# Feed-forward up projections as seven half products for eight, with each feed-forward in an up phase and a down phase

## What is computed

```python
h = x + concat(pool_mixer, rg_lru) @ w_out            # first block: mixer
h = h + square(relu(rms_norm(h) @ w_up)) @ w_down     # feed-forward one,   1024 -> 4096 -> 1024
h = h + sigmoid(rms_norm(h) @ w_ple_gate + b) * (p @ w_ple_proj)
h = rms_norm(h)
# second block
h = h + 0.5 * rms_norm((silu(a) * b) @ ffn1_w_out)    # a, b = split(rms_norm(h) @ ffn1_w_in), 1024 -> 2 x 2816
h = h + rms_norm(mixer(h))                            # dilated attention and an S5 state space model
h = h + 0.5 * rms_norm((silu(a) * b) @ ffn2_w_out)    # feed-forward three, like two
```

## Time and profile before

| | |
|---|---|
| median of 3 runs | 3018.67 us (3018.64 to 3019.09) |
| profiled execution, span from first to last instruction | 3016.7 us |
| TensorE | 2998.1 us busy (99%), 14144 matmuls |
| VectorE, ScalarE, GpSimd | 45%, 29%, 14% busy |
| granted TensorE clock | 1.000 |
| DMA | 69 GB/s on the mean |

### The profile page before, as it was taken

How to read it: one execution, slowest core, us unless ns; L and a number is a source line. 1 busy time by engine, 2 the same in 40 slices (tenths; PEclk the granted TensorE clock), 3 DMA queues, 4 the chain that set the end, 5 groups by cost and what they waited for, 6 DMA issues and landing times.

```text
span 3016.7 us, 36793 instructions
## 1 busy us (share of the span) xinstructions
PE 2998.1 (99%) x14144; PEld 2465.9 (82%) x14144; DVE 1351.8 (45%) x1735; ACT 870.4 (29%) x1328; POOL 408.9 (14%) x1004
## 2 busy tenths in 40 slices
PE   8999999999999999999999999999999999999999
PEld 7788888888888888888888888887788888888887
DVE  5854444444445453333333353346655333333335
ACT  6524122112214352111111143136744111111112
POOL 0010000000000001988860010012100000000000
PEclk9999999999999999999999999999999999999999
DMA  3131111111112121222221132212131111111113
GB/s 131 41 108 53 56 56 49 35 56 56 42 42 68 45 85 49 75 97 100 89 82 42 49 133 84 78 63 98 55 133 70 49 49 49 58 54 42 42 49 133
DMA packets 54553, 206.98 MB, mean 69 GB/s; under 512 B 7232, under 2 KB 8000, under 8 KB 52144
## 3 DMA queue, kind: packets, MB, share of 16 engines
q1 hardware_dynamic: 38736, 140.53, 13.9%
q0 software_dynamic: 15712, 65.02, 5.9%
HBM read 173.15 MB, written 31.20 MB: 68 GB/s over the span
## 4 chain that ended last, share of the span: by engine, by line
PE 97%; DVE 2%; ACT 1%; issue 0%; DMA 0%; SPq 0%; DVEq 0%; ACTq 0%
PE ps L128 30%; PE ps L130 30%; PE ps L129 30%; PE ps L1976 1%; PE ps L268 1%; PE ps L1991 1%; PE ps L1950 1%; PE ps L340 0%; PE ps L1626 0%; DVE acc L179 0%; ACT junk L200 0%; PE ps L1659 0%; DVE acc L187 0%; PE ps L1667 0%; ACT junk L166 0%; PE ps L1639 0%
## 5 line engine op out<-in xcount | busy, mean ns | idle before, releaser
L128 PE MATMUL ps<-region_a,region_b 128*128 128x512 f32 x1664 | 654.9, 394 | 1.0 <-DVE region_a L227 1.0
L130 PE MATMUL ps<-region_a,region_b 128*128 128x512 f32 x1664 | 648.0, 389 | 0.0
L129 PE MATMUL ps<-region_a,region_b 128*128 128x512 f32 x1664 | 647.5, 389 | 0.0
L128 PE MATMUL ps<-region_b,region_a 128*128 128x512 f32 x1088 | 428.2, 394 | 0.1
L130 PE MATMUL ps<-region_b,region_a 128*128 128x512 f32 x1088 | 424.9, 391 | 0.0
L947 DVE TENSOR_TENSOR acc<-acc,ps 128x1024 f32<-128x1024 f32 x240 | 292.9, 1220 | 294.0 <-PE ps L130 294.0
L129 PE MATMUL ps<-region_b,region_a 128*128 128x512 f32 x1088 | 424.5, 390 | 0.0
L123 DVE TENSOR_TENSOR region_b<-raw,region_b 128x1024 fp32r<-128x1024 f32 x176 | 216.2, 1244 | 348.5 <-ACT region_b L119 348.2
L128 PEld LDWEIGHTS ps<-region_a,region_b 128*128 128x128 f32 x1664 | 312.5, 188 | 66.4 <-issue 1.8
L130 PEld LDWEIGHTS ps<-region_a,region_b 128*128 128x128 f32 x1664 | 312.4, 188 | 65.2
L129 PEld LDWEIGHTS ps<-region_a,region_b 128*128 128x128 f32 x1664 | 312.6, 188 | 64.3 <-issue 1.7
(11 more groups left out here) (302 smaller groups left out, 3233.6 us busy)
## 6 DMA issues: line engine op xcount, KB each, us to landing
raw<-stream SPq DMA_DIRECT2D x252, 512.0 KB, 3.3
ssm_row<-ssm_mid POOLq DMA_DIRECT2D x8, 1632.0 KB, 7.3
x_mid<-acc POOLq DMA_DIRECT2D x24, 512.0 KB, 3.1
ssm_mid<-made_osc POOLq DMA_DIRECT2D x8, 1024.0 KB, 4.3
ssm_mid<-made_out POOLq DMA_DIRECT2D x8, 608.0 KB, 3.4
acc<-x SPq DMA_DIRECT2D x8, 512.0 KB, 8.1
rold<-x POOLq DMA_DIRECT2D x16, 256.0 KB, 3.7
old_a<-x_mid POOLq DMA_DIRECT2D x8, 512.0 KB, 8.2
```

The costliest lines, as they stand in the source:

```text
L128: nc.tensor.matmul(psum, lhs(0), rhs(0), start=first, stop=False)
L129: nc.tensor.matmul(psum, lhs(0), rhs(1), start=False, stop=False)
L130: return nc.tensor.matmul(psum, lhs(1), rhs(0), start=False, stop=last)
```

## The change

Class `Feed` is replaced by class `Quick`, and each feed-forward has two phases.

**Up phase.** Two units of weights (a pair; with gate, the gate's and the other's 128 features) are a 2 x 2 matrix of blocks (two halves of the 1024 inputs, two units), the rows are two halves of inputs by two halves of rows. Their product is made with seven half products for eight: seven products of 4 x 3 matmuls for a pair, from sums of weight blocks (`weight_sum` on VectorE in feed-forward two, `weight_sum_pool` on GpSimd in one and three; four for a pair) and from sums of the blocks of `Z` (once for a feed-forward: `mixed_first_dve` and the functions behind it). `join_dve` adds the products into the four results, seven additions of 128x512 for a pair. Each of the seven has its own hi and lo of 128x512 (`weight_hi`, `weight_lo`, L856) in one of 7 slots, six products ahead. The slots lie where `acc` was, so `acc` is first stored (`keep_rows`). Finished activations are stored to HBM (`hid`).

**Down phase.** For rows 0 to 511 and then for rows 512 to 1023, all hidden tiles are read back with their weights (`hid_raw`, `raw`), split (`down_hi`, `down_lo`), and summed in PSUM over all hidden tiles, so that `acc` is written once.

**What moves with it.** The factors of the tables are hooks of products 26, 40, 46 and 52 of the up phase of feed-forward two. `hid_raw` lies where GpSimd builds the tables, so SyncE waits for `s_out` ahead of the first load of that down phase.

```diff
-            step = lambda N, d: lambda: norm_pe_step(pe, N, 0, d)
-            feed_pe(pe, mlp, n_mlp, {...
+            quick_up_pe(pe, mlp)
+            quick_down_pe(pe, mlp, turns(mlp, n_ple))
...
+                order = [(0, 1), (0, 2), (1, 1), (1, 2), (0, 5), (1, 5), (0, 6), (1, 6), (0, 7), (1, 7), (0, 4), (0, 3),
+                         (2, 1), (1, 4), (2, 2), (1, 3)]
+                for p in range(2, pairs):
+                    order += [(p, 6), (p, 7), (p, 4), (p, 5)] + ([(p + 1, 1), (p + 1, 2)] if p + 1 < pairs else []) + [(p, 3)]
...
+        def quick_up_pe(pe, F):
+            N = F.norm
+            for i, (p, q) in enumerate(F.order):
+                pe.wait_ge(*F.at("lo", i + 1))
+                earlier = [j for j in range(i) if F.ring_at(j) == F.ring_at(i)]
+                pe.wait_ge(*(F.emptied(earlier[-1]) if earlier else F.banks_free[i]))
+                for k in range(4):
...
+                    elif p == 0:
+                        pe.wait_ge(*F.at("zlo", 4 * {5: 0, 6: 1, 7: 2, 4: 3}[q] + k + 1))
+                    last = products(ps[:, F.bank_at(i), :], lambda h: up_slots[:, i % SLOTS_UP, h, k * P:(k + 1) * P],
+                                    lambda h: F.moving(q, k, h), k == 0, k == 3)
+                    if i == 2 and k == 2:
+                        mixed_turn_pe(pe, F, 0)
+                    if i == 3:
+                        mixed_turn_pe(pe, F, k + 1)
...
+        def quick_up_dve(dve, F, hooks={}):
+            for i in range(4, F.N):
+                if i + AHEAD < F.N:
+                    weight_step_dve(dve, F, i + AHEAD)
+                if i > 4:
+                    up_dve_then(dve, F, i - 1)
+                if i not in (6, 7, 8, 9):
+                    up_dve_now(dve, F, i)
+                if i == F.N - 4:
+                    down_lo(dve, F, 0)
+                hooks.get(i, lambda: None)()
...
+        def copy_act(act, F, i):
+            p, q = F.order[i]
+            if p >= 2:
+                act.wait_ge(*F.at(f"stored{p % 2}", F.stored_by * (p // 2)))
...
+            def down(kk):
+                th, k = divmod(kk, F.n)
+                if kk < 2:
...
+                    for cond in F.hid_free:
+                        sp.wait_ge(*cond)
...
+            for p in range(F.pairs):
+                pair(p)
+                if p >= 3:
+                    store(p - 3)
+            down(0)
+            down(1)
+            store(F.pairs - 3)
+            store(F.pairs - 2)
+            store(F.pairs - 1)
...
+        ffn1.hid_free = [(s_out, 32 * NB)]
...
-            feed_on_dve(dve, ffn1, mix2_norm_hooks(dve), {(1, 1): lambda: ssm_angle_dve(dve)},
-                        {1: lambda: ssm_growth_dve(dve), 3: lambda: ssm_inverse_dve(dve),
-                         5: lambda: ssm_factors_dve(dve)})
+            weight_lo(dve, ffn1, 2)
+            weight_lo(dve, ffn1, 3)
+            quick_start_dve(dve, ffn1)
+            quick_up_dve(dve, ffn1, {26: lambda: ssm_angle_dve(dve), 40: lambda: ssm_growth_dve(dve),
+                                     46: lambda: ssm_inverse_dve(dve), 52: lambda: ssm_factors_dve(dve)})
```

More of the change, by code:

```diff
@@ L684, in dve_out1 @@
                 hooks.get(g - NT, lambda: None)()
[L687 to L695, removed]
-                self.base, self.sem = {}, {}
-                take(self, dict(up=2 * self.nU * n, ge=halves if gated else 0, ue=0 if gated else halves, sq=halves,
-                                hi=halves, lo=halves, dn=NT * (n - 1), de=NT * (n - 1), fr=1))
+        SLOTS_UP, AHEAD, AHEAD_DOWN = 7, 6, 3
@@ L737, in down_slot @@
[L737 to L754, removed]
@@ L1051, in first_lo, with ended, down_done, all_stored @@
-        def first_lo(dve, F, us=range(2)):
-            for u in us:
-                make_lo(dve, F.n0 + u, F.W[:, u], (F.n0 + u) % 2)
-        U_MLP = U_OUT + 8
-        mlp = Feed(D_FF1 // P // CHUNK, False, A, B, U_MLP, [(w_out.done, NT)] * 2, True)
-        U_PLE = mlp.last_n
+            def ended(self):
+                return self.at("done", self.N)
+            def down_done(self, kk):
+                return self.at("done", self.N + kk + 1)
+            def all_stored(self, par):
+                return self.at(f"stored{par}", self.stored_by * self.pairs // 2)
@@ new lines, in emptied, with tile_bank @@
+            def emptied(self, i):
+                p, q = self.order[i]
+                if q == 1:
+                    return self.at("copied", self.n_copy[p, "P1"])
+                if q == 4 and self.gated:
+                    return self.at("out", self.n_out[p, 4])
+                return self.at("joined", self.n_join[p, {2: "C11", 6: "U2", 7: "U3", 4: "C21", 5: "C22", 3: "C12"}[q]])
+            def tile_bank(self, th, i):
+                return (4, 6, self.bases[0], self.bases[1])[i] if th == 0 else (6, 0, 2, 4)[i]
@@ new lines, in weight_sums_pool, with weight_step_dve @@
+        def weight_sums_pool(pool, F):
+            pool.wait_ge(*F.norm.at("tr", 2 * KD))
+            for p, s in ((0, 1), (1, 1), (0, 2), (1, 2), (0, 3), (0, 4), (1, 3), (1, 4)):
+                weight_sum_pool(pool, F, p, s)
+            for p in range(2, F.pairs):
+                for s in (1, 2, 3, 4):
+                    weight_sum_pool(pool, F, p, s)
+        def weight_step_dve(dve, F, i):
+            p, q = F.order[i]
+            if F.sums_by == "dve":
+                if p >= 2 and q in (1, 2):
+                    weight_sum(dve, F, p, q)
+                if q == 3 and 2 <= p + 1 < F.pairs:
+                    weight_sum(dve, F, p + 1, 3)
+                if p >= 2 and q == 5:
+                    weight_sum(dve, F, p, 4)
+            weight_lo(dve, F, i)
@@ new lines, in quick_up_pe @@
+        def quick_up_pe(pe, F):
+            N = F.norm
+            for i, (p, q) in enumerate(F.order):
[3 more added lines that the diff above has]
+                for k in range(4):
+                    if p == 0 and q in (1, 2):
+                        pe.wait_ge(*N.at("lo", 4 * (q - 1) + k + 1))
+                    elif p == 0 and q == 3:
+                        pe.wait_ge(*N.at("lo", KD + k + 1))
+                    elif p == 0:
[6 more added lines that the diff above has]
+                        mixed_turn_pe(pe, F, k + 1)
+                last.then_inc(F.sem["done"], 1)
+                if i == 3:
+                    for d in range(5, KD):
+                        mixed_turn_pe(pe, F, d)
```

1178 lines of the change are left out of this document (715 added, 463 removed).

## The result

The change makes the kernel slower: 3149.6 us (3146.9 to 3151.0, four runs) against 3018.7 before, ratio 1.0433 [1.0418, 1.0447]. Forecast was 3080 (3035 to 3120). The direction was right, the size was not: +131 us for +62. The profiled execution has a span of 3145.0 us, so 128.3 are to be explained, where the forecast had 61.8. Two executions ran far longer at a full granted clock and are left out of the medians: one of kernel 8 (6994.4 us) and one of the kernel before in the same comparison (8754.2).

The account below looks back on a forecast made before the run. TensorE was taken to bound the kernel, busy for 99% of the span. Removed matmuls -163.2, starts +74.0 and the table wait +151.0 sum to +61.8 us on a 3016.7 span: median 3080 us, range 3035 to 3120.

Parts of the forecast that it names:

- matmuls removed: Up phases: a pair costs 84 matmuls, not 96; 720 fewer at 0.2267 us, -163.2 us.
- starts: Start of each feed-forward: TensorE waits behind VectorE's queue, 17.2 + 33.0 + 23.8 = +74.0 us, bounds 50 and 100.
- tables: Feed-forward two: TensorE idle from 1527.4 to 1678.4 until GpSimd's tables are done and stored, +151.0 us.
- Bound, steady phase: TensorE bounds the kernel; in the steady up phase a matmul takes 0.2267 us and nothing is added on the path.
- The table wait: TensorE stops at product 150; its bank's copy needs a store queued behind loads that wait for the tables: +151.0 us.
- full block: Rival: each VectorE instruction with two SBUF inputs takes its whole 0.69 us from GpSimd; pace 0.62, 3109 us, chance 0.10.
- Products 9 and 10: 2.1 each time: Last waits listed at each feed-forward's start: 2.1 us in front of products 9 and 10 together.
- so I charge nothing: TensorE's clock after idle stretches: granted clock 1.00 behind the 7.2 us wait at the start, so no cost.
- slow TensorE: Rival: each idle stretch is followed by one product at half pace, 2.7 us each; 3091 us, chance 0.08.
- In the down phase ... Also hidden: Down phase: a tile needs 1.5 x 512 KB in 5.44 us of TensorE, 512 KB land in 3.3; no cost.
- The end: Kernel's end: keeps its 6.5 us or so behind the last matmul.
- four half-pace products: Slow-clock case at the starts: only four products not hidden behind VectorE, 4 x 2.7 = 11 us, in the range's top.

Follow-up runs that it names:

- kernel 8: Changed kernel with tables early, hidden tiles read into region B, stores ahead of loads (feed-forwards two, three), kept rows later, product 10's weights split early: 2974.3 us.
- Kernels 1 to 3: Changed kernel with one edit each: tables' factors earlier, 3095.9 us; feed-forward two's hidden tiles read back into region B, 3014.1; its stores ahead of down-phase loads, 3136.1.
- kernel 1: Changed kernel with the tables' factor steps moved from products 26, 40, 46, 52 to 17, 22, 24, 26: 3095.9 us.
- kernel 6: Changed kernel with the split of product 10's weights right behind that of product 9, in all three feed-forwards: 3136.8 us.
- kernel 5: Changed kernel with the weight sums of feed-forwards one and three moved from GpSimd to VectorE: 3145.4 us.
- kernel 7: Changed kernel with extra matmuls, results overwritten, filling TensorE's waits in front of products 2, 4 and 6: 3151.0 us.
- kernels 8 and 9: kernel 8 at 2974.3 us, and the same with the weight sums of feed-forwards one and three on VectorE, at 2973.6 us.
- kernel 4: Changed kernel with the kept rows read back behind down tile 8 in feed-forwards two and three, not when the up phase ends: 3134.7 us.

## Why the prediction was too low, step by step

| term, us | forecast | trace |
|---|---|---|
| matmuls removed | -163.2 | -163.2 |
| starts | +74.0 | +109 (84.4 of waits, 22 at half pace, 3 restarts) |
| tables | +151.0 | +143.3 (141.6 and 1.7 at half pace) |
| turn to the down phase | 0 | +27 (9.3, 10.3, four of 0.7 to 0.9, half pace 4.0) |
| stages between | 0 | +7 (2.5, 1.0, 1.4, half pace 1.8) |
| not placed | | +5 |
| sum | +61.8 | +128.3 |

Of the 66.5 that the forecast lacks, 35 are the starts, 27 the turn to the down phase and 7 the stages between; the tables give 8 back.

- **Bound, steady phase:** right. 0.2265 us for a matmul; no wait of TensorE from 1165 to 1525.
- **The table wait:** right in mechanism, place and size. Kernels 1 to 3 show each part: the tables' end (88.9 where 88 was expected), the buffer, the store behind the loads. GpSimd's pace was 0.76, where the rows had given 0.73 and a full block 0.62. The Trainium skill (SBUF — State Buffer, Who interferes with whom) says that VectorE's instructions with two SBUF inputs contend with GpSimd's reads, and calls the shared port pair an exclusive lock; the full block it spells out for VectorE's two-port modes, and the prediction carried it over. The trace agrees on who contends (kernel 1), and not on a block for the whole of an instruction: 0.76 for 0.62 in the tables, and in the 6.19 us of the four subtractions (2.49 alone) GpSimd made 3.7 sums of 1.29, which one behind the other would take 7.3.
- **The starts: the step that failed.** "Products 9 and 10: 2.1 each time" was the last entry, as if the start were over. The third pair's load waits for product 10's split, and joins wait behind five splits on VectorE: 23.4 us (kernel 6). The other 22 that were missing are half pace, the next point. The count of VectorE's instructions up to there was near in sum, 61.0 for 74.0, and in part by luck: too low in front of product 4 in one and three, 9.2 for 5.2, where GpSimd's sums, priced at nothing, hold VectorE (kernel 5), and too high in front of products 6 and 8, 15.9 for 31.6.
- **"so I charge nothing" (TensorE's clock):** wrong as a reading. The only wait of before stood where the clock held, and I took one case as a rule. The rival "slow TensorE" had the mechanism. The Trainium skill (TensorE: Matmul & The Clock Gate, Part 1) says that TensorE's clock is 1.2 GHz after idling, and the trace agrees: 0.50 in 287.2 to 292.0. Of its 22 us at the starts those in front of product 12, some 17, only become waits when they are taken away (kernel 7); the 5 behind product 12's wait count in full (kernels 8 and 9). So what counts up to there is that the start as a whole is VectorE's, and longer than I counted.
- **"In the down phase ... Also hidden":** wrong. I compared one tile's load with one tile's time and left out the 4 MB of kept rows that GpSimd's queue starts in the same moment (kernel 4); 15 us measured.
- **The end:** right, the last matmul ends at 3138.6, 6.5 us before the span does.
- **Range:** the top of 3120 came from the full block and four half-pace products. It held no case in which the starts cost over 100, though their bounds were 50 and 100 and the loads' costs nothing.

What stays open: 5 us of the account, and when the clock falls behind a wait of under 3 us.

## What to carry to other kernels

When a change gives an engine a dense block of work, follow its queue until it is idle again, not until the last instruction that you expected; what is behind a load that waits for a release inside the block comes late as well. For each load that a change adds, list all other transfers that start in the same moment, on every queue. A stall that is hundreds of matmuls long can hang on one buffer's address: ask what else could hold it before giving up the change (3149.6 became 3014.1, and 2969.6 with the rest).

## What the hardware showed

- A GpSimd sum of 128x512 takes 1.7 us beside VectorE's subtractions with two inputs in SBUF for 1.29 without them, and these take 1.55 each for 0.62 alone: both lose. An addition of VectorE with one input in PSUM keeps 0.68 in the same microseconds.
- Behind the 9.19 us wait at 287.18 eleven matmuls took 4.8 us at a clock of 0.50; behind the 1.38 us wait at 314.44 the next ones kept 0.23 each.
- While the DMA engines are busy for all of their time (394 to 416 GB/s), the hidden tile's load issued at 2892.2 landed at 2904.0, 12 us for the usual 3.9.
